# GDN stage: the solve's second product goes out through ScalarE, and the output's low half moves behind the solve's last sums on VectorE

## Chip, core and metric
One Trainium2 chip, one of its NeuronCores. The metric is the time of one execution on the device in microseconds (us), as the median of several runs; lower is better. Engines in the profile: PE is TensorE's matmul and PEld its weight load, DVE is VectorE, ACT is ScalarE, POOL is GpSimd, SP is SyncE, which issues the loads.

## What is computed
Two blocks of a language model run one after the other on a sequence of 512 tokens of width 1024, in float32. The change touches one mixer of the second block, the gated delta rule (GDN), with 8 query and key heads and 16 value heads of width 128 and chunks of 64 tokens:

```python
L = where(strict, einsum(kb, k) * decay, 0)
T = triangular_solve(eye + L, eye)         # a 64 x 64 unit lower triangle for each head and chunk
u, w = T @ vb, T @ (kb * exp(g))
for each chunk:
    v_new = u_n - w_n @ state
    o     = q_n @ state + a_n @ v_new
    state = state * gl_n + k_n^T @ v_new
y = (rmsnorm(o, norm_w) * silu(z)) @ w_out
```

## The kernel before
All float32 products with weights are made from a high and a low half (fp32r): hi x hi, hi x lo, lo x hi. The weights come in blocks of 128 x 1024; SyncE loads a block, ScalarE makes its high half (`split_hi`, L261), VectorE the low one (`split_lo`, L267). The output of the mixer is split in the same way before it is multiplied with `a_w_out`: ScalarE writes `o_hi` (`high`, L2819), VectorE `o_lo` (`low`, L3017 to L3020).

The GDN stage goes through the 8 query/key heads in turns: one "first", six "mid" and one "last" (`gdn_turns`, L2397). Each engine has its own list of instructions for a turn, in an order written out by hand, and the engines meet at semaphores whose values the class `Steps` counts: `Steps.done(name)` raises, `Steps.after(name, turn)` is what another engine waits for. The names in a list must come in the order in which the engine does them.

A turn (j) computes, beside its own head, parts of two others: VectorE and ScalarE prepare the next head's convolution (`conv`, L2966 and L2722), and from the second turn on the head before (p) is normed, gated, split (`normed`, `gated`, `high`, `low`) and multiplied with the output weights (`out_tile` on TensorE, L2515, and on VectorE, L2979). TensorE's large products of the projections (L281) and of the output (L2526 to L2528) are cut into units that a table, `GDN_BESIDE` (L2344), puts behind the small products of the solve, so that TensorE has work while the other engines evict a result. The solve has these steps, `a` being the lower 64 partitions and `b` the upper ones, each product 32 or 48 matmul records of 64 x 64 (`halves`, L2490, all recorded under L2495):
- `f` into the first banks (4 and 7), `g` into the second banks (5 and 6), one after the other; behind them the units of "c" (a quarter of a projection in the middle turns, nothing in the last).
- ScalarE copies `f` out (`fa`, `fb`), VectorE `g` (`ga`, `gb`, L3092), and then adds the identity to the same banks (`ha`, `hb`).
- `f2` needs `fb` and `gb`. ScalarE copies one half of it (`f2a`), VectorE the other (`f2b`, L3096).
- `v` needs `f2a` and `f2b`; VectorE adds it to `ha` and `hb` (`va`, `vb`, L3103). In the last turn output unit O0 follows `v`; in the middle turns two projection units do.
- `y` needs `vb`; behind it come, in the middle turns, a projection unit and O0; then `at` and the four 128-token steps of the recurrence.

O0 is the first output unit, and waits for `lo_1`, the end of `low` (L2519). `low` waits for ScalarE's `high`. On VectorE `low` stands between `f2b` and `va`; ahead of `ga` stand the next head's first convolution and `gated`. Helpers record their callers' instructions under one line: `tt` is L3030 on VectorE, `run` is L2826 on ScalarE.

The lines that order VectorE around the solve:

```python
pe("g")                                                     # L3090
... ga, gb: dve.tensor_copy(G.m[r, :], src[r])              # L3092
... ha, hb: bank + identity
pe("f2"); f2b; splits("vc")
if p is not None: low(p)                                    # L3099
pe("v"); own("hb"); va, vb                                  # L3103
splits("f"); conv(1), conv(2); pe("at")
```

Of the kernel before, what the change touches and what calls it, by code (L numbers as in the profile page):

```python
# [6 lines left out]
ACT = mybir.ActivationFunctionType  # L7
# [5 lines left out]
P = 128  # L13
# [104 lines left out]
def first_and_second_block(nc, a, out):  # L118

    with ExitStack() as ctx:  # L120
        def sem(name):
            return ctx.enter_context(nc.semaphore(name))
# [1246 lines left out]
        class Gla:  # L1369
            b0, t0 = BASE["gla"]  # L1370
            a_lr = tile("gla_a_lr", 8)
            q, k, v, g = ([gla_qkvg[:, n * T:n * T + T] for n in range(n0, n1)] for n0, n1 in ((0, 2), (2, 4), (4, 8), (8, 12)))
            u = [tile(f"gla_u{n}", (21, 30, 31, 32)[n]) for n in range(4)]
            zb, az, cum, rel = ([tile(f"gla_{n}{m}", 33 + 2 * k + m) for m in range(2)]
                                for k, n in enumerate(("zb", "az", "cum", "rel")))
# [10 lines left out]
            pe = Steps(sem("gla_pe"), ["z0", "z1", "vt0", "vt1", "kt0", "kt1", "vt2", "kv00", "kv01", "vt3", "sc0", "sc1", "sc2", "kv10", "kv11", "sc3",  # L1386
                                       "o0", "o1", "sum0", "sum1", "o2", "pw3", "pw2", "o3", "sum2", "sum3", "pw1", "pw0"])
# [443 lines left out]
        class Dsa:  # L1831
# [12 lines left out]
            p, pT = [tile(f"dsa_p{m}", 8 + m) for m in range(4)], [tile("dsa_pT0", 45), sumsq]  # L1844
# [7 lines left out]
            pe = Steps(sem("dsa_pe"), ["sw_kk", "sw_qi0", "sw_qi1", "wt"] + [f"is{t}{h}" for t in range(1, TT) for h in range(IDX_HEADS)]  # L1852
                       + ["vt0", "vt1"])
# [432 lines left out]
        class Gdn:  # L2286
            b0, t0 = BASE["gdn"]
            o_hi, o_lo = ([tile(f"gdn_o_{n}{h}", k + h, dt=F32R) for h in range(2)] for n, k in (("hi", 0), ("lo", 2)))
            gb, dec, eg_row = ([tile(f"gdn_{n}{h}", k + h) for h in range(2)] for n, k in (("gb", 4), ("dec", 6), ("eg_row", 8)))
# [73 lines left out]
        class GdnNext:  # L2363

            pe = Steps(sem("gdn_next_pe"), ["sums"])
# [16 lines left out]
        class GdnTurn:  # L2382
# [4 lines left out]
                       + [n for t in range(TT) for n in (both([f"ks{t}"]) if t else []) + both([f"vn{t}"])  # L2387
                          + [f"{n}{t}_{h}" for h in range(2) for n in (["o", "ds"] if t < TT - 1 else ["o"])]]
                       + ["sums"])
            act = Steps(sem("gdn_act"), ["kc", "vc_0", "vc_1", "fa", "fb", "f2a", "c", "y", "bt", "ct"]  # L2390
                        + [n for t in range(TT) for n in both([f"vn{t}"])] + both(["sq", "oc"]))
            dve = Steps(sem("gdn_dve"), both(["m", "in", "E", "at"]) + [f"{n}{k}" for k in range(GDN_STEPS) for n in ("ta", "tb")]
                        + ["P", "PT", "ga", "gb", "ha", "hb", "f2b", "va", "vb", "at"]
                        + [n for t in range(TT) for n in (both([f"r{t}"]) if t else []) + (both([f"s{t}"]) if t < TT - 1 else [])])
            pool = Steps(sem("gdn_pool"), both(["qd"]) + ["eye"] + both(["kd"]))

# [17 lines left out]
        def first(h):  # L2414
            return bank[(4, 7)[h]]

        def second(h):
            return bank[(5, 6)[h]]
# [60 lines left out]
        def gdn_pe(pe, run):  # L2479
# [81 lines left out]
            def turn(j, p, i, at):  # L2561
# [45 lines left out]
                halves("f", (first(0)[a], half_of(G.X, a), of_E(a, a)), (first(1)[b], half_of(G.X, b), of_E(b, b)))  # L2607
                halves("g", (second(0)[a], of_E(a, a), half_of(G.X, a)), (second(1)[b], of_E(b, b), half_of(G.X, b)))
                beside("c")
                act("fb")  # L2610
                dve("gb")
                halves("f2", (first(0)[a], half_of(G.m, a), half_of(G.F, a)), (first(1)[b], half_of(G.m, b), half_of(G.F, b)),
                       (first(0)[b], half_of(G.X, a), of_E(a, b)))
                beside("f2")
# [88 lines left out]
        def gdn_act(act, after):  # L2703
# [117 lines left out]
            def turn(j, p, i, at):  # L2821
                pe, dve, pool, own = ((lambda n, S=S: act.wait_ge(*S.after(n, j))) for S in (H.pe, H.dve, H.pool, H.act))
                odd, more = 1 - gdn_odd(at), at.kind != "last"

                def run(step, out, src, f, **kw):
                    act.activation(out, src, f, **kw).then_inc(*H.act.done(step))  # L2826

                def splits(point):
                    for n in GDN_SPLITS[at.kind].get(point, "").split():
                        split(at, i, n)  # L2830

                def halves(x):
                    return x.rearrange("p (c x) -> p c x", x=INV_PART)
                if p is not None:
                    inverse_roots(p)
                pe("kt")
                run("kc", G.k_tok[:], second(0)[:], ACT.Copy)
                splits("start")
                for h in range(2):
                    pe(f"vt_{h}")  # L2840
                    run(f"vc_{h}", G.v_tok[h][:], second(1 - h)[:], ACT.Copy)
                splits("vc")
                if p is not None:
                    for h in range(2):
                        gate(h, *gdn_gate(at, i, h)[:3])
                if more:
                    pool("qd_1")
                    conv(0, j + 1, i, at, odd)
                    conv(1, j + 1, i, at, odd)
                a, b = slice(0, P // 2), slice(P // 2, P)  # L2850
                pe("f")
                run("fa", G.F[a, :], first(0)[a], ACT.Copy)
                run("fb", G.F[b, :], first(1)[b], ACT.Copy)
                splits("f")
                pe("f2")
                run("f2a", G.F2[a, :], first(0)[a], ACT.Copy)
                run("c", G.CY[a, :], first(0)[b], ACT.Copy)
                if more:
                    silu(0, i, at, odd)
                    conv(2, j + 1, i, at, odd)  # L2860
                if p is not None:
                    high(p)
                splits("f2")
                pe("y")
                run("y", G.CY[b, :], first(0)[b], ACT.Copy)
                run("bt", G.T[b, :, b], halves(first(1)[b]), ACT.Copy)
                if more:
                    silu(1, i, at, odd)
                    squares(j + 1, odd, p)
                    conv(3, j + 1, i, at, odd)  # L2870
                else:
                    for h in range(2):
                        gate(h, at.through(f"z{h}", i), at.bank(f"z{h}"), (tile_free, BANKS + at.tile[f"z{h}"]))
                pe("at")
                run("ct", G.T[a, :, b], halves(first(1)[a]), ACT.Copy)
                if more:
                    sums(j + 1)
                for t in range(TT):
                    if not more and t == TT - 1:
                        act.preload_act_table_set("natural_log_exp_and_others")  # L2880
                    for h in range(2):
                        pe(f"vn{t}_{h}")
                        if t >= 2:
                            pe(f"o{t - 2}_{h}")
                            pe(f"ds{t - 2}_{h}")
                        run(f"vn{t}_{h}", G.W1[h][:, (1 + t % 2) * P:(2 + t % 2) * P], first(h)[:, (t % 2) * P:(t % 2) * P + P], ACT.Copy,
                            scale=G.beta[:, bass.ds((j * 2 + h) * TT + t, 1)])
                    splits(f"vn{t}")
                    if more and t == 0:
                        for u in (2, 3):  # L2890
                            silu(u, i, at, odd)
                    if more and t == 1:
                        act.preload_act_table_set("natural_log_exp_and_others")
                        roots(j + 1)
                        decays(j + 1)
                    if more and t == 2:
                        gate_rows(j + 1)
                for h in range(2):
                    pe(f"o{TT - 1}_{h}")
                    run(f"sq_{h}", G.W3[h][:], second(h)[:], ACT.Square)  # L2900
                for h in range(2):
                    if more:
                        act.wait_ge(*N.pool.after("n_q", j + 1))
                    run(f"oc_{h}", G.sq[h][:], second(h)[:], ACT.Copy, scale=par[:, R_GDNN:R_GDNN + 1])
                splits("end")
# [18 lines left out]
        def gdn_dve(dve):  # L2924
# [92 lines left out]
            def low(p):  # L3017
                for h in range(2):
                    dve.wait_ge(*GdnOut.act.after(f"hi_{h}", p))
                    dve.tensor_tensor(G.o_lo[h][:], G.sq[h][:], G.o_hi[h][:].bitcast(F32), ALU.subtract).then_inc(*GdnOut.dve.done(f"lo_{h}"))  # L3020

            def turn(j, p, i, at):
# [3 lines left out]
                def done(step):  # L3026
                    return H.dve.done(step)

                def tt(step, out, x, y, op):
                    dve.tensor_tensor(out, x, y, op).then_inc(*done(step))  # L3030

                def splits(point):
                    for n in GDN_LOWS[at.kind].get(point, "").split():
                        split(at, i, n)
# [53 lines left out]
                if p is not None:  # L3088
                    gated(p, [gdn_gate(at, i, h)[3] for h in range(2)])
                pe("g")  # L3090
                for n, r, src in (("ga", a, second(0)), ("gb", b, second(1))):
                    dve.tensor_copy(G.m[r, :], src[r]).then_inc(*done(n))  # L3092
                for n, r, src in (("ha", a, second(0)), ("hb", b, second(1))):
                    tt(n, halves(G.V1[r, :]), halves(src[r]), eye(r), ALU.add)
                pe("f2")
                dve.tensor_copy(G.F2[b, :], first(1)[b]).then_inc(*done("f2b"))  # L3096
                splits("vc")
                if p is not None:
                    low(p)  # L3099
                pe("v")  # L3100
                own("hb")
                for n, r, src in (("va", a, second(0)), ("vb", b, second(1))):
                    tt(n, G.V[r, :], G.V1[r, :], src[r], ALU.add)  # L3103
                splits("f")
                if more:
                    conv(1, j + 1, i, at, odd)
# [870 lines left out]
```

## Time and profile before

| | |
|---|---|
| median of 3 runs | 2735.11 us (2734.95 to 2738.89) |
| the profiled execution's own time | 2736.56 us |
| its span, first to last instruction | 2734.8 us |
| mean granted TensorE clock | 0.998 of full speed |
| busy: TensorE, VectorE, ScalarE, GpSimd | 98%, 65%, 47%, 33% of the span |
| GDN stage's turns | about 1865 to 2389 us of the span |

How to read it: the span is what the profile covers; the device time is 1.8 us longer. "Busy" says how much of the span an engine has an instruction in flight; a matmul counts as busy from its start to its modelled end, so consecutive ones overlap. The chain that ended last is followed back from the last instruction through whatever released each step, and so shows whose time adds up to the span. In a timeline each row has the start, the length and the instruction; "x2" is two merged instructions, and the bracket is the idle time of the engine ahead of it with the releaser that the semaphores suggest. "issue" is idle time for which the profile names no releaser.

### The profile page before, as it was taken

To read this page: it belongs to the slowest core of one execution; us is meant where nothing else is said; L and a number is where in the kernel's file an instruction comes from. 1 tells how busy PE (TensorE), PEld (TensorE's weight loads), DVE (VectorE), ACT (ScalarE), POOL (GpSimd) and SP (SyncE) were. 2 spreads that over 40 slices of the span, in tenths; PEclk is the share of its full clock that TensorE was granted. 3 is DMA by queue.
4 is the path that set the end of the run, shared out by engine and by line. 5 is a ranking of instruction groups with operands and counts; after the bars stand their busy time and mean duration, and the time that the engine had idled before them with its cause. 6 is when DMAs were issued, how large, how long until landed. Compare 5 with 4: busy or idle time off the path is not lost.

```text
span 2734.8 us, 40987 instructions
## 1 busy us (share of the span) xinstructions
PE 2681.2 (98%) x15550; PEld 2223.8 (81%) x15550; DVE 1787.3 (65%) x2641; ACT 1274.7 (47%) x2008; POOL 899.6 (33%) x751
## 2 busy tenths in 40 slices
PE   8999999999999999999999999999999999899998
PEld 6998888789888898887788998877777777777777
DVE  7974336569753687635956887348777777676664
ACT  4542232445323453223554543345555555467775
POOL 5520013136431264403733545104422222122232
PEclk9999999999999999999999999999999999999999
DMA  5343332223553325533213256322222222122222
GB/s 144 87 123 93 96 82 78 82 80 101 170 159 94 96 85 157 175 96 85 78 31 90 83 145 181 106 70 71 78 70 70 70 70 63 44 78 65 66 62 70
DMA packets 484876, 255.94 MB, mean 94 GB/s; under 512 B 17843, under 2 KB 478422, under 8 KB 484710
## 3 DMA queue, kind: packets, MB, share of 16 engines
q1 hardware_dynamic: 484534, 253.40, 32.4%
q8 instruction: 111, 1.82, 0.3%
q14 instruction: 55, 0.45, 0.1%
q10 hardware_dynamic: 176, 0.27, 0.0%
HBM read 251.51 MB, written 2.13 MB: 93 GB/s over the span
## 4 chain that ended last, share of the span: by engine, by line
PE 89%; DVE 6%; ACT 2%; issue 1%; POOL 1%; DMA 0%; SPq 0%; DVEq 0%; ACTq 0%; POOLq 0%
PE bank L281 60%; PE bank L978 12%; PE bank L2495 1%; PE bank L2526 1%; PE bank L2528 1%; DVE w_lo L267 1%; PE bank L2527 1%; DVE dsa_work L2191 1%; PE bank L3435 1%; PE bank L3427 1%; DVE small L2185 1%; PE bank L2640 1%; PE bank L3460 1%; DVE gdn_blocks L3030 1%; PE bank L1569 1%
## 5 line engine op out<-in xcount | busy, mean ns | idle before, releaser
L267 DVE TENSOR_TENSOR w_lo<-w_raw,w_hi 128x1024 fp32r<-128x1024 f32 x365 | 463.1, 1271 | 463.2 <-ACT w_hi L261 443.8
L281 PE MATMUL bank<-x_hi,w_hi 128*128 128x512 f32 x1808 | 737.7, 408 | 6.0 <-DVE w_lo L267 4.2
L281 PE MATMUL bank<-x_lo,w_hi 128*128 128x512 f32 x1808 | 707.8, 391 | 0.6 <-DVE x_lo L623 0.6
L281 PE MATMUL bank<-x_hi,w_lo 128*128 128x512 f32 x1808 | 707.5, 391 | 0.0
L261 ACT ACTIVATE w_hi<-w_raw 128x1024 fp32r<-128x1024 f32 x349 | 366.9, 1056 | 489.7 <-PE bank L281 440.7
L281 PEld LDWEIGHTS bank<-x_hi,w_hi 128*128 128x128 f32 x1808 | 340.4, 188 | 88.1 <-issue 16.5
L281 PEld LDWEIGHTS bank<-x_hi,w_lo 128*128 128x128 f32 x1808 | 340.1, 188 | 74.3
L281 PEld LDWEIGHTS bank<-x_lo,w_hi 128*128 128x128 f32 x1808 | 341.1, 189 | 68.1 <-DVE x_lo L623 3.9
L468 POOL TENSOR_TENSOR sumsq<-sumsq,sq 128x512 f32<-128x512 f32 x56 | 90.3, 1613 | 711.8 <-ACT sq L456 711.2
L281 PE MATMUL bank<-h_hi,w_hi 128*128 128x512 f32 x768 | 300.3, 391 | 0.0
L281 PE MATMUL bank<-h_hi,w_lo 128*128 128x512 f32 x768 | 299.0, 389 | 0.0
L281 PE MATMUL bank<-h_lo,w_hi 128*128 128x512 f32 x768 | 298.8, 389 | 0.0
L281 PEld LDWEIGHTS bank<-h_hi,w_hi 128*128 128x128 f32 x768 | 144.2, 188 | 30.6
L281 PEld LDWEIGHTS bank<-h_hi,w_lo 128*128 128x128 f32 x768 | 144.2, 188 | 30.5
L281 PEld LDWEIGHTS bank<-h_lo,w_hi 128*128 128x128 f32 x768 | 144.2, 188 | 29.4
L978 PE MATMUL bank<-t_hi,w_hi 128*128 128x256 f32 x512 | 146.1, 285 | 0.7 <-DVE w_lo L1192 0.7
L978 PE MATMUL bank<-t_lo,w_hi 128*128 128x256 f32 x512 | 144.8, 283 | 0.0
L978 PE MATMUL bank<-t_hi,w_lo 128*128 128x256 f32 x512 | 144.8, 283 | 0.0
L716 POOL TENSOR_TENSOR sumsq<-sumsq,ada_hi 128x512 f32<-128x512 f32 x48 | 62.1, 1293 | 160.9 <-DVE ada_hi L702 160.9
L978 PE MATMUL bank<-x_hi,w_hi 128*128 128x256 f32 x384 | 109.2, 284 | 0.3
L978 PE MATMUL bank<-x_lo,w_hi 128*128 128x256 f32 x384 | 108.7, 283 | 0.0
L978 PE MATMUL bank<-x_hi,w_lo 128*128 128x256 f32 x384 | 108.6, 283 | 0.0
(542 smaller groups left out, 5070.1 us busy)
## 6 DMA issues: line engine op xcount, KB each, us to landing
w_raw<-in_ffn_wi_dram SPq DMA_DIRECT2D x176, 512.0 KB, 3.8
w_raw<-in_ffn_wo_dram SPq DMA_DIRECT2D x64, 512.0 KB, 3.5
w_raw<-in_ada_w_dram SPq DMA_DIRECT2D x48, 512.0 KB, 4.8
w_raw<-in_a_w_in_dram SPq DMA_DIRECT2D x48, 512.0 KB, 4.0
w_raw<-in_b_w_in_dram SPq DMA_DIRECT2D x32, 512.0 KB, 4.0
w_raw<-in_ffn_wo_dram SPq DMA_DIRECT2D x32, 384.0 KB, 3.1
w_raw<-in_even_w_in_dram SPq DMA_DIRECT2D x16, 512.0 KB, 4.0
w_raw<-in_a_w_out_dram SPq DMA_DIRECT2D x16, 512.0 KB, 3.5
```

The lines of the kernel that those rows point to most:

```text
L261: act.activation(w_hi[b % SPLIT][:], w_raw[raw % RAW][:], ACT.Copy).then_inc(w_hi_done, 1)
L267: dve.tensor_tensor(w_lo[s][:], w_raw[raw_of(b) % RAW][:], w_hi[s][:].bitcast(F32), ALU.subtract).then_inc(w_lo_done, 1)
L281: mm = pe.matmul(out, lhs[:, w], rhs(kt), start=first and kk == 0 and m == 0, stop=last and kk == len(kts) - 1 and m == 2)
L468: pool.tensor_tensor(sumsq[:], sumsq[:], sq[k % 2][:], ALU.add).then_inc(sum_added, 1)
L716: pool.tensor_tensor(dst, x, y, ALU.add).then_inc(ada_added, 1)
L978: mm = pe.matmul(out, lhs[:, w], rhs[:, k, :], start=first and k == 0 and m == 0, stop=k == 3 and m == 2, skip_group_check=True)
L1569: pe.matmul(out[:], w_hi[b % SPLIT][:, w], h_hi[:, x], start=first and kt == kts[0], stop=False)
L2185: dve.max(S.top8, w).then_inc(*s.done(f"top{t}_{k}"))
L2191: dve.match_replace(w, S.top8, w, TAKEN).then_inc(*s.done(f"out{t}_{k}"))
L2495: mm = pe.matmul(out[:, c * INV_PART:(c + 1) * INV_PART], lhs(c), rhs(c), start=True, stop=True)
L2526: pe.matmul(out[:], w_hi[s][:, x], G.o_hi[h][:], start=h == 0, stop=False)
L2527: pe.matmul(out[:], w_hi[s][:, x], G.o_lo[h][:], start=False, stop=False)
```

## The change
ScalarE, not VectorE, copies the product `g` out of its banks: `ga` and `gb` follow `fa` and `fb` on ScalarE. TensorE waits for the one semaphore value `gb` of ScalarE ahead of `f2`. VectorE waits for ScalarE's `gb` ahead of `ha`. On VectorE `low` moves from ahead of `va` to behind `vb`.

```diff
--- before.py
+++ after.py
@@ -2387,10 +2387,10 @@
                        + [n for t in range(TT) for n in (both([f"ks{t}"]) if t else []) + both([f"vn{t}"])
                           + [f"{n}{t}_{h}" for h in range(2) for n in (["o", "ds"] if t < TT - 1 else ["o"])]]
                        + ["sums"])
-            act = Steps(sem("gdn_act"), ["kc", "vc_0", "vc_1", "fa", "fb", "f2a", "c", "y", "bt", "ct"]
+            act = Steps(sem("gdn_act"), ["kc", "vc_0", "vc_1", "fa", "fb", "ga", "gb", "f2a", "c", "y", "bt", "ct"]
                         + [n for t in range(TT) for n in both([f"vn{t}"])] + both(["sq", "oc"]))
             dve = Steps(sem("gdn_dve"), both(["m", "in", "E", "at"]) + [f"{n}{k}" for k in range(GDN_STEPS) for n in ("ta", "tb")]
-                        + ["P", "PT", "ga", "gb", "ha", "hb", "f2b", "va", "vb", "at"]
+                        + ["P", "PT", "ha", "hb", "f2b", "va", "vb", "at"]
                         + [n for t in range(TT) for n in (both([f"r{t}"]) if t else []) + (both([f"s{t}"]) if t < TT - 1 else [])])
             pool = Steps(sem("gdn_pool"), both(["qd"]) + ["eye"] + both(["kd"]))
 
@@ -2607,8 +2607,7 @@
                 halves("f", (first(0)[a], half_of(G.X, a), of_E(a, a)), (first(1)[b], half_of(G.X, b), of_E(b, b)))
                 halves("g", (second(0)[a], of_E(a, a), half_of(G.X, a)), (second(1)[b], of_E(b, b), half_of(G.X, b)))
                 beside("c")
-                act("fb")
-                dve("gb")
+                act("gb")
                 halves("f2", (first(0)[a], half_of(G.m, a), half_of(G.F, a)), (first(1)[b], half_of(G.m, b), half_of(G.F, b)),
                        (first(0)[b], half_of(G.X, a), of_E(a, b)))
                 beside("f2")
@@ -2851,6 +2850,9 @@
                 pe("f")
                 run("fa", G.F[a, :], first(0)[a], ACT.Copy)
                 run("fb", G.F[b, :], first(1)[b], ACT.Copy)
+                pe("g")
+                run("ga", G.m[a, :], second(0)[a], ACT.Copy)
+                run("gb", G.m[b, :], second(1)[b], ACT.Copy)
                 splits("f")
                 pe("f2")
                 run("f2a", G.F2[a, :], first(0)[a], ACT.Copy)
@@ -3088,19 +3090,18 @@
                 if p is not None:
                     gated(p, [gdn_gate(at, i, h)[3] for h in range(2)])
                 pe("g")
-                for n, r, src in (("ga", a, second(0)), ("gb", b, second(1))):
-                    dve.tensor_copy(G.m[r, :], src[r]).then_inc(*done(n))
+                act("gb")
                 for n, r, src in (("ha", a, second(0)), ("hb", b, second(1))):
                     tt(n, halves(G.V1[r, :]), halves(src[r]), eye(r), ALU.add)
                 pe("f2")
                 dve.tensor_copy(G.F2[b, :], first(1)[b]).then_inc(*done("f2b"))
                 splits("vc")
-                if p is not None:
-                    low(p)
                 pe("v")
                 own("hb")
                 for n, r, src in (("va", a, second(0)), ("vb", b, second(1))):
                     tt(n, G.V[r, :], G.V1[r, :], src[r], ALU.add)
+                if p is not None:
+                    low(p)
                 splits("f")
                 if more:
                     conv(1, j + 1, i, at, odd)
```

## Rows read from the trace of the kernel before

**Rows 1.** The page's chain that ended last, share of the span by engine.
```profile
PE 89%; DVE 6%; ACT 2%; issue 1%; POOL 1%; DMA 0%; SPq 0%; DVEq 0%; ACTq 0%; POOLq 0%
```

**Rows 2.** Waits in the GDN stage: engine line, releaser; us in total, times, longest.
```profile
PE bank L2495 <- issue: 7.6, 6, 1.6
...
PE bank L2495 <- DVE gdn_W L3030: 1.8, 6, 0.3
```

**Rows 3.** TensorE's timeline, a middle turn: start us, length us, instruction, idle before.
```profile
2015.34 0.40 PE L281 MATMUL bank<-x_hi,w_lo 128*128 128x512 f32 x1
2016.93 0.27 PE L2495 MATMUL bank<-gdn_W,gdn_W 64*64 64x64 f32 x2 [1.20 <-issue]
...
2019.28 0.40 PE L281 MATMUL bank<-x_hi,w_lo 128*128 128x512 f32 x1
2019.61 1.15 PE L2495 MATMUL bank<-gdn_W,gdn_W 64*64 64x64 f32 x32
...
2023.31 0.39 PE L281 MATMUL bank<-x_hi,w_lo 128*128 128x512 f32 x1
2024.01 0.24 PE L2495 MATMUL bank<-gdn_W,gdn_W 64*64 64x64 f32 x1 [0.31 <-DVE gdn_W L3030]
...
2026.60 0.39 PE L2526 MATMUL bank<-gdn_o_hi,w_hi 128*128 128x512 f32 x1
```

**Rows 4.** VectorE's timeline, the same stretch.
```profile
2015.43 1.40 DVE L3092 COPY gdn_W<-bank 64x512 f32<-64x512 f32 x2
2016.87 1.41 DVE L3030 TENSOR_TENSOR gdn_W<-bank,ident 64x512 f32<-64x512 f32 x2
2018.19 0.69 DVE L3096 COPY gdn_W<-bank 64x512 f32<-64x512 f32 x1
...
2021.13 1.29 DVE L3020 TENSOR_TENSOR gdn_o_lo<-gdn_sq,gdn_o_hi 128x512 fp32r<-128x512 f32 x2 [1.00 <-ACT gdn_o_hi L2819]
2022.46 1.40 DVE L3030 TENSOR_TENSOR gdn_W<-gdn_W,bank 64x512 f32<-64x512 f32 x2
```

**Rows 5.** ScalarE's timeline, the same stretch.
```profile
2013.25 1.21 ACT L2826 ACTIVATE gdn_W<-bank 64x512 f32<-64x512 f32 x2 [4.48 <-PE bank L2495]
2014.49 1.06 ACT L261 ACTIVATE w_hi<-w_raw 128x1024 fp32r<-128x1024 f32 x1
2018.14 1.21 ACT L2826 ACTIVATE gdn_W<-bank 64x512 f32<-64x512 f32 x2 [2.59 <-PE bank L2495]
...
2020.48 1.14 ACT L2819 ACTIVATE gdn_o_hi<-gdn_sq 128x512 fp32r<-128x512 f32 x2
```

**Rows 6.** Pieces of the chain of waits, first turn and a middle one.
```profile
1885.70 3.11 PE bank L2495 x64
1888.81 2.08 PE bank L281 x6
...
2012.13 2.01 PE bank L2495 x64
```

**Rows 7.** Waits in the GDN stage, the two that the first turn has too.
```profile
PE bank L2495 <- DVE gdn_P L3076: 3.0, 2, 2.2
...
PE bank L2495 <- DVE gdn_W L3096: 1.7, 2, 0.9
```

**Rows 8.** Timelines of TensorE, VectorE and ScalarE, last turn.
```profile
2358.22 0.27 PE L2495 MATMUL bank<-gdn_W,gdn_W 64*64 64x64 f32 x2 [1.55 <-DVE gdn_W L3092]
...
2360.27 1.15 PE L2495 MATMUL bank<-gdn_W,gdn_W 64*64 64x64 f32 x32 [0.89 <-DVE gdn_W L3096]
2362.58 0.47 PE L2526 MATMUL bank<-gdn_o_hi,w_hi 128*128 128x512 f32 x1 [1.16 <-issue]
...
2361.19 1.29 DVE L3020 TENSOR_TENSOR gdn_o_lo<-gdn_sq,gdn_o_hi 128x512 fp32r<-128x512 f32 x2 [1.02 <-ACT gdn_o_hi L2819]
...
2355.78 1.21 ACT L2826 ACTIVATE gdn_W<-bank 64x512 f32<-64x512 f32 x2 [11.30 <-PE bank L2495]
```

**Rows 9.** Busy us of each engine and TensorE's granted clock (PEclk), one stretch.
```profile
core 0: us, PE busy (x) PEld busy (x) DVE busy (x) ACT busy (x) POOL busy (x), PEclk, DMA share, GB/s
1887.00:1888.00 1.00, 1.00 (x24) 1.00 (x23) 0.75 (x1) 0.84 (x2) 1.00 (x1) 0.50 0.07 16
```


## The prediction

> **What bounds the kernel now.** I read first the page's chain of waits by engine: TensorE has 89% of the span [rows 1], so a microsecond counts only where TensorE stands idle. Then I read, for the GDN stage, who waited for whom: before the lines of the solve's small products (L2495) TensorE is idle six times for 7.6 us under the name "issue" and six times for 1.8 us behind VectorE's L3030 [rows 2]. Third, the timelines of the three engines through one middle turn. There are eight turns (first, six middle ones, last), and the six middle ones repeat this pattern.
>
> On TensorE the last matmul of the work beside "c" starts at 2015.34, and f2 only at 2016.93, 1.20 us idle; later y starts at 2024.01, 0.31 us idle [rows 3]. In the same stretch VectorE copies ga and gb from 2015.43 to 2016.83, that is, late, because the convolution and the gating stand ahead of them, and f2 starts 0.10 us after gb [rows 3, 4]. So I read "issue" here as the wait for gb. The second idle stretch: va and vb end at 2023.86 and y starts 0.15 us later; they are late because `low` stands ahead of them and itself waits 1.00 us for ScalarE's high half [rows 3, 4]. ScalarE was done with fb at 2014.46 and, but for one weight split, is idle until f2 is through at 2018.1 [rows 5].
>
> **Step 1, ga and gb on ScalarE (middle turns).** Two VectorE copies of 0.70 us go; two ScalarE copies of the same shape come. That form is in the trace: fa and fb take 1.21 us together [rows 5]. f and g together end at 2012.13 + 2.01 = 2014.14, before fb ends [rows 5, 6], so nothing is waited for and gb is done at 2014.46 + 1.21 = 2015.67. With 0.10 to 0.15 us for the wake-up (what rows 3 and 4 show from VectorE; from ScalarE to this product no row shows it, so bounds 0.0 and 0.3) f2 starts at 2015.8. Unhindered it would start 0.33 after the last matmul beside it has started, as v does (2019.61 after 2019.28), at 2015.67 [rows 3]. Gain 16.93 - 15.8 = 1.1 us. In the first middle turn the idle time is 1.6 instead of 1.2 (the longest in [rows 2]) and ScalarE is as early there, so 1.5. Together 5 x 1.1 + 1.5 = 7.0 us.
>
> What is queued behind on ScalarE: the weight split of 1.06 us goes from 2014.49 to 2015.7, ends at 2016.8, and f2a, which needs f2's end at about 2016.95, loses nothing. silu, the copy beside it and `high` follow f2a as before, so the high halves end at 21.62 - 1.1 = 2020.5 [rows 5]. Who waits for gb on VectorE: the two additions ha and hb, now from 2015.75 instead of 2016.87, end 2017.15; f2b until 2017.85 [rows 4]. TensorE reaches v at 19.61 - 1.1 = 2018.5, so v isn't held, with 0.65 us to spare.
>
> The Trainium skill speaks against this move: "ScalarE: Activation LUTs", section Rules for kernel authors, sends simple elementwise operations (maximum, addition, product) to VectorE and budgets about 0.3 us plus 0.83 ns per element for a ScalarE instruction. An estimate from that page is 0.72 us for 512 elements, 1.45 for the two, where this trace has 1.21 for the two.
>
> **Step 2, `low` behind va and vb (middle turns).** v now ends at 2018.5 + 1.15 = 2019.65; VectorE has ended its weight split (2018.88 to 2020.13 before, 1.25 us, now from 2017.85) at 2019.1 and waits for v 0.6 us. va and vb: 2019.7 to 2021.1. TensorE reaches y, without a wait, at 0.33 after the matmul that started 2023.31, less 1.1: 2022.55 [rows 3, 4]. So y's whole delay goes, 24.01 - 23.64 = 0.37 us, six times: 2.2 us. `low` runs from 2021.1, the high halves being there since 2020.5, to 2022.4, where it ended at 2022.42 before. The first output product, which needs it, starts at 26.60 - 1.5 = 2025.1 [rows 3], 2.7 us later. Everything that VectorE has behind (a weight split, two convolutions, the copy of `at`) begins at 2022.4 instead of 2023.86, 1.5 us earlier, as much as TensorE gains, so no later wait opens. GpSimd, which waits for vb, starts the next decays earlier and is off the path. No DMA is added; SyncE's loads wait for the splits that come no later. Middle turns: 7.0 + 2.2 = **9.2 us gained**.
>
> **Step 3, the first turn.** No `low`, no gating, and the work beside "c" hides ga and gb either way. What is idle there is 0.85 us before v, behind f2b, which follows f2 itself [rows 7]. Zero: the cover is the six matmuls, 1.6 us and more; without it the price would be as in the last turn, 0.1 us.
>
> **Step 4, the last turn.** Nothing stands beside "c" there and no convolution ahead of ga, so VectorE copies as soon as g is done, and f2 starts at 2358.22. ScalarE ends fb at 2355.78 + 1.21 = 2356.99, so gb ends at 2358.2 and f2 starts at 2358.3: 0.1 us lost instead of anything gained [rows 8]. And here the first output product follows v directly. Now it waits 1.16 us for `low`, which ends at 2362.48, and starts at 2362.58. In the changed order: v ends at 2360.27 + 0.1 + 1.15 = 2361.5, va and vb take 1.40 as in the middle turns (to 2363.0), `low` 1.29 (to 2364.35), the product starts at 2364.45 [rows 4, 8]. y then follows it directly. **1.9 us lost**, all on the path.
>
> **Step 5, TensorE's clock in the last turn.** The idle time between v and that product grows to 64.45 - 61.5 = 2.9 us. In the first turn TensorE was idle for 2.2 us before f [rows 7], and then the granted clock went to 0.50 of full speed (1.2 instead of 2.4 GHz) [rows 9]. The price is in the chain of waits: f and g took 3.11 instead of 2.01 us and the six matmuls beside them 2.08 instead of 15.74 - 14.14 = 1.60 [rows 3, 6], together 1.6 us. None of the idle times of 1.2 to 1.6 us had this effect. With 2.9 us I take the fall as likely, at 1.5 us, since a part of the slow stretch may lie in the idle time. Bounds: 0 (no fall) and 1.6; a gain is excluded, as a clock can't be granted above full.
>
> **Sum.** 9.2 - 1.9 - 1.5 = 5.8 us gained. The profiled execution (2736.56 us, span 2734.8) becomes 2730.8; the median of the runs, 2735.1, becomes **2729.3 us**, 0.21% less. A measurement of this kernel tells about 0.2% (5.5 us) from no change, so the forecast lies just beyond that bound.
>
> With the Trainium skill's budget ("ScalarE: Activation LUTs", Rules for kernel authors) gb would end at 2015.9 and f2 start at 2016.0: 0.25 us less in each middle turn and the last, 1.7 us in all.
>
> **Rivals.**
> (a) The clock doesn't fall in the last turn: 9.2 - 1.9 = 7.3 gained, 2727.8 us. For it: the last turn of before has three idle stretches of 0.9 to 1.6 us, one after another, which kept f2, v and the product at their usual pace [rows 8]. Against it: 2.9 us is longer than the 2.2 that went before a fall. 22%.
> (b) The change doesn't do what it says in the middle turns: the 1.20 us is TensorE's own issue, as the view names it, or v is held by f2b so that the lead is gone before v. Then only y's 2.2 us are won and 3.4 lost: 2736.3 us. Against it: in the last turn the same idle time is put to VectorE's copy, with the same pattern [rows 2, 8]. 10%.
> (c) ScalarE is no faster at ga and gb than VectorE is: 1.40 us for the two instead of 1.21 [rows 4, 5]. Then gb ends 0.2 us later in the six middle turns and the last one, 1.3 less gained, 2730.6 us. Against it: the same shape from the same kind of bank, fa and fb, takes 1.21. 4%. The Trainium skill's budget, in the section named above, would be a case of this rival, with the 1.7 us given beside the sum.
> (d) Slower: in the middle turns `low` is now behind v, and the first output product waits for `low` as it does in the last turn. From rows, 2.7 us lie between. If VectorE comes to `low` more than 2.7 us later than worked out (because the high halves are late on ScalarE behind ga and gb), TensorE stands in each of six turns. It decides from 2.7 + (9.2 - 3.4) / 6 = 3.7 us on; at 5 us late, 6 x 2.3 - 5.8 = 8 us lost, 2743 us. Against it: `high` ends half a microsecond before VectorE asks. 4%.
> The forecast has 60%.
>
> **The numbers.** Range 2725.8 to 2733.0 us: from (a) less 2 us for the wake-up's lower bound and the scatter of the median (the runs lie between 2734.95 and 2738.89), to 2729.3 with (c), the wake-up at 0.3 (1 us) and the same scatter; (b) and (d) are left out, 14%, and some of the tails. Faster by over 0.2%: all but a little of (a), and somewhat over half of the forecast, which is 0.3 us beyond the bound: 0.54. Within 0.2%: the rest of it, (b) and (c): 0.42. Slower: 0.04.
>
> **What the changed profile would show.** Step 1: no idle time over 0.2 us before f2 in the middle turns, four ScalarE copies in a row, VectorE's L3092 gone. Step 2: none before y, `low` without the 1.00 us of waiting. Each middle turn is 1.5 us shorter. Step 4: 2.9 us idle before L2526 in the last turn, where 1.16 was. Step 5: a granted clock of 0.50 just behind it. Wrong would be: an idle stretch that is new in the middle turns, before v or before L2526, or an "issue" of 1.2 us that stays.

## The result and the profile after

The change made the kernel slower: 2741.43 us median (2740.71 to 2744.14, 16 runs) against 2736.39 us for the kernel before (16 runs); ratio 1.0019 with a 95% interval of 1.0013 to 1.0026. The profiled span grew from 2734.8 to 2739.1 us. The predicted 2729.3 us and the range up to 2733.0 are missed.

Where the 4.3 us of span are, in the profiled executions, by the starts of three matmul groups (the second turn's and the last turn's product kk, L2485, and the sum of squares behind the stage, L503):

| | before | after | predicted change |
|---|---|---|---|
| up to the second turn's kk | 1924.17 | 1923.67 | 0 |
| six middle turns, each | 68.80 | 69.03 | -1.5 |
| last turn, kk to L503 | 66.40 | 69.90 | +3.4 |
| from there to the end | 331.4 | 331.4 | 0 |

The last turn came out as worked out. The middle turns should have given 9.2 us and cost 1.4. The page's chain that ended last, as in [rows 1], shows where to look: VectorE's share grew from 6% to 10% and TensorE's fell.

```profile
PE 87%; DVE 10%; issue 1%; ACT 1%; POOL 1%; DMA 0%; SPq 0%; DVEq 0%; POOLq 0%; ACTq 0%
```

The waits in the GDN stage (as [rows 2]: us in total, times, longest):

```profile
PE bank L2634 <- DVE gdn_W L3142: 5.4, 7, 0.9
...
PE bank L2526 <- issue: 2.9, 1, 2.9
...
PE bank L2526 <- DVE gdn_kT L2975: 1.9, 6, 0.3
...
PE bank L2639 <- ACT gdn_T L2825: 1.2, 6, 0.2
```

The two groups of [rows 2], f2's six stretches of 7.6 us and y's six of 1.8, are gone. In their place TensorE is idle at three points of each middle turn: ahead of output unit O1 (L2526), where it waits for VectorE's convolution of k; ahead of the first tile's product (L2639), where it waits for one of ScalarE's copies into the tile T; and ahead of the second tile's (L2634; the seventh time is in the first turn), where it waits for VectorE's copy of the state. One middle turn on TensorE, as in [rows 3]:

```profile
2027.63 0.50 PE L2526 MATMUL bank<-gdn_o_hi,w_hi 128*128 128x512 f32 x1 [0.31 <-DVE gdn_kT L2975]
...
2030.61 0.68 PE L2639 MATMUL bank<-gdn_v_tok,gdn_T 128*128 128x128 f32 x4 [0.21 <-ACT gdn_T L2825]
...
2035.79 0.71 PE L2634 MATMUL bank<-gdn_W,gdn_kT 128*128 128x128 f32 x4 [0.82 <-DVE gdn_W L3142]
```

0.31 + 0.21 + 0.82 us are idle here, where 1.20 + 0.31 were. That is less, and still the turn is 0.23 us longer: a bracket counts from the modelled end of the last matmul and leaves out that the first ones behind it come slower (the second of O1's matmuls starts 0.33 us after the first, the third 0.24 after the second). By the starts of the matmuls, against the same turn of experiment 3, which has none of these waits, the three points put what follows back by 0.5, 0.4 and 0.8 us, 1.7 in sum; the two of the kernel before by 1.1 and 0.4, 1.5 in sum.

ScalarE did what was expected. As in [rows 5], but with the two new copies behind the two old ones, it does four in 2.45 us from 2012.73 with no wait between them, and the high halves end at 2020.0:

```profile
2012.73 2.45 ACT L2825 ACTIVATE gdn_W<-bank 64x512 f32<-64x512 f32 x4 [4.48 <-PE bank L2495]
...
2018.86 1.14 ACT L2818 ACTIVATE gdn_o_hi<-gdn_sq 128x512 fp32r<-128x512 f32 x2
```

VectorE in the same stretch, to be read against [rows 4]:

```profile
2015.28 1.41 DVE L3032 TENSOR_TENSOR gdn_W<-bank,ident 64x512 f32<-64x512 f32 x2 [0.27 <-ACT gdn_W L2825]
...
2019.18 1.40 DVE L3032 TENSOR_TENSOR gdn_W<-gdn_W,bank 64x512 f32<-64x512 f32 x2 [0.64 <-PE bank L2495]
2020.62 2.38 DVE L3022 TENSOR_TENSOR gdn_o_lo<-gdn_sq,gdn_o_hi 128x512 fp32r<-128x512 f32 x2
2022.92 2.31 DVE L267 TENSOR_TENSOR w_lo<-w_raw,w_hi 128x1024 fp32r<-128x1024 f32 x1
2025.26 2.32 DVE L2975 SCALAR_TENSOR_TENSOR gdn_kT<-bank,par,gdn_kT 128x511 f32<-128x511 f32 x3
```

Up to vb all is on the forecast's schedule: ha and hb wait 0.27 us for gb, v is waited for 0.64 us (0.6 was said), va and vb take 1.40. Then `low` (L3022) takes **2.38 us for its two instructions, not 1.29**, and the weight split behind it **2.31, not 1.23**. That is 2.17 us of VectorE in each middle turn, against a lead of 1.5. What runs beside them is GpSimd, in whose timeline the decays of the next head (`front`, released by vb) begin 0.04 us after `low`:

```profile
2020.66 3.48 POOL L3172 TENSOR_TENSOR gdn_dec<-gdn_gb,not_above 128x512 f32<-128x512 f32 x2 [23.82 <-DVE gdn_W L3032]
2024.10 3.02 POOL L3175 TENSOR_TENSOR gdn_dec<-gdn_dec,gdn_cols 128x512 f32<-128x512 f32 x2
```

In the kernel before the same instructions of GpSimd and VectorE stood like this:

```profile
2023.94 3.58 POOL L3171 TENSOR_TENSOR gdn_dec<-gdn_gb,not_above 128x512 f32<-128x512 f32 x2 [26.57 <-DVE gdn_W L3030]
2027.49 2.03 POOL L3174 TENSOR_TENSOR gdn_dec<-gdn_dec,gdn_cols 128x512 f32<-128x512 f32 x2
...
2023.89 1.23 DVE L267 TENSOR_TENSOR w_lo<-w_raw,w_hi 128x1024 fp32r<-128x1024 f32 x1
2025.15 2.31 DVE L2973 SCALAR_TENSOR_TENSOR gdn_kT<-bank,par,gdn_kT 128x511 f32<-128x511 f32 x3
```

There the split had begun 0.05 us ahead of GpSimd and kept its 1.23 us; it was GpSimd's first instruction that was stretched (2.32 us of the 3.58 for the two; the median of the stage's sixteen is 1.29). And behind the split came the convolutions, which read one operand from a bank and one from SBUF, and ran beside GpSimd at their usual 2.31 us for three. The change put `low`, both of whose inputs are in SBUF, between vb and the split.

The last turn, as in [rows 8] and [rows 9]:

```profile
2361.40 1.15 PE L2495 MATMUL bank<-gdn_W,gdn_W 64*64 64x64 f32 x32 [0.92 <-DVE gdn_W L3097]
2365.41 0.69 PE L2526 MATMUL bank<-gdn_o_hi,w_hi 128*128 128x512 f32 x1 [2.87 <-issue]
...
2366.00:2367.00 1.00, 1.00 (x4) 0.81 (x3) 0.45 (x1) 0.00 (x0) 0.00 (x0) 0.50 0.00 0
```

TensorE was idle 2.87 us between v and O0 (2.9 was forecast), and the granted clock was at 0.50 behind it, from 2365.5 to 2368.9.

### The profile page after: what moved, and what is told of

It is laid out like the page before. It is cut to its first block, busy times and chain, and to the rows that moved or that the text cites. A ratio compares the mean times of both kernels' runs of the same rounds, so it can differ in the third digit from the quotient of the medians.

```text
span 2739.1 us, 40995 instructions
## 1 busy us (share of the span) xinstructions
PE 2684.0 (98%) x15550; PEld 2224.8 (81%) x15550; DVE 1791.6 (65%) x2625; ACT 1284.9 (47%) x2024; POOL 904.5 (33%) x751
## 3 DMA queue, kind: packets, MB, share of 16 engines
HBM read 251.51 MB, written 2.13 MB: 93 GB/s over the span
## 4 chain that ended last, share of the span: by engine, by line
PE 87%; DVE 10%; issue 1%; ACT 1%; POOL 1%; DMA 0%; SPq 0%; DVEq 0%; POOLq 0%; ACTq 0%
PE bank L281 59%; PE bank L978 12%; DVE w_lo L267 2%; DVE gdn_vT L2975 1%; PE bank L2495 1%; DVE dsa_work L2191 1%; PE bank L3436 1%; PE bank L3428 1%; DVE small L2185 1%; PE bank L2526 1%; PE bank L3461 1%; DVE gdn_blocks L3032 1%; PE bank L2528 1%; PE bank L1569 1%; PE bank L2527 1%
## 5 line engine op out<-in xcount | busy, mean ns | idle before, releaser
L267 DVE TENSOR_TENSOR w_lo<-w_raw,w_hi 128x1024 fp32r<-128x1024 f32 x365 | 472.3, 1298 | 461.3 <-ACT w_hi L261 442.1
```

The costliest lines, as they stand in the source:

```text
L267: dve.tensor_tensor(w_lo[s][:], w_raw[raw_of(b) % RAW][:], w_hi[s][:].bitcast(F32), ALU.subtract).then_inc(w_lo_done, 1)
```

## The theories

Theory 1 ("the port" in the expectations): a VectorE instruction with two inputs in SBUF and a GpSimd instruction don't run at the same time; the one that comes second waits until the other has ended. The runs can show this wait, not the circuit behind it. Theory 2: the copies that ScalarE took over stretch what stands beside them, or hold up ScalarE's queue. The experiments take one half of the change at a time, and move only the moment at which GpSimd is released. In the kernel as it stands the first turn releases GpSimd's decays by `PT`, an earlier point, so their data allow any later one.

Turn lengths (us) are read as in the table above, each from the one profiled execution; the median is over all runs, and the ratio is to the runs of the kernel before on the same chip.

| kernel | median us | ratio, 95% interval | middle turn | last turn |
|---|---|---|---|---|
| before | 2736.39 | | 68.80 | 66.40 |
| the change | 2741.43 | 1.0019 (1.0013 to 1.0026) | 69.03 | 69.90 |
| e1 copies only | 2729.68 | 0.9972 (0.9962 to 0.9983) | 67.64 | 66.67 |
| e2 low only | 2747.78 | 1.0038 (1.0025 to 1.0052) | 70.16 | 70.37 |
| e3 GpSimd behind low | 2732.24 | 0.9981 (0.9972 to 0.9990) | 67.23 | 71.33 |
| e4 last turn as before | 2739.35 | 1.0006 (0.9997 to 1.0015) | 68.99 | 66.64 |
| e5 both repairs | 2728.92 | 0.9972 (0.9962 to 0.9982) | 67.23 | 68.52 |
| e6 before, GpSimd early | 2743.17 | 1.0024 (1.0014 to 1.0034) | 69.87 | 66.38 |
| e7 split ahead of low | 2743.19 | 1.0020 (1.0011 to 1.0029) | 69.01 | 71.40 |
| e8 GpSimd behind at | 2735.05 | 0.9992 (0.9983 to 1.0001) | 67.98 | 69.88 |
| e9 = e5 again | 2728.42 | 0.9966 (0.9954 to 0.9978) | 67.22 | 68.45 |
| e10 = e1 again | 2730.40 | 0.9975 (0.9966 to 0.9985) | 67.59 | 68.83 |

## Experiment 1: only the copies move

The edit, against the changed kernel:

```diff
                 splits("vc")
+                if p is not None:
+                    low(p)
                 pe("v")
...
                     tt(n, G.V[r, :], G.V1[r, :], src[r], ALU.add)
-                if p is not None:
-                    low(p)
```

> Only the first half of the change: ga and gb on ScalarE, low stays ahead of va. Theory 1 (the port): in the middle turns the moved low lets GpSimd's decays, released by vb, start together with low, and VectorE's instructions with two inputs in SBUF and GpSimd's wait for each other, 2.2 us in each middle turn. Here vb is followed by the weight split as before, so no instruction of VectorE is stretched: low 1.29 us, the split 1.23; the middle turn is 1.1 to 1.2 us shorter than 68.7, f2's idle time is gone, y's 0.3 stays; the last turn is as before within 0.1 us. In all 7 to 7.5 us less than before, 2729 us. Theory 2 (the copies on ScalarE stretch what stands beside them, or hold its queue so that the high halves and the squares come late): low and the split are stretched here too, and the time is that of before or above, 2736 us or more.

Measured: 2729.68 us, middle turn 67.64, as theory 1 had it. VectorE, GpSimd and TensorE in a middle turn:

```profile
2018.62 1.29 DVE L3022 TENSOR_TENSOR gdn_o_lo<-gdn_sq,gdn_o_hi 128x512 fp32r<-128x512 f32 x2 [0.97 <-ACT gdn_o_hi L2818]
...
2021.38 1.23 DVE L267 TENSOR_TENSOR w_lo<-w_raw,w_hi 128x1024 fp32r<-128x1024 f32 x1
...
2021.43 3.57 POOL L3172 TENSOR_TENSOR gdn_dec<-gdn_gb,not_above 128x512 f32<-128x512 f32 x2 [25.48 <-DVE gdn_W L3032]
...
2021.50 0.24 PE L2495 MATMUL bank<-gdn_W,gdn_W 64*64 64x64 f32 x1 [0.31 <-DVE gdn_W L3032]
```

`low` takes 1.29 us and the split 1.23, with ScalarE's copies in place: the copies stretch neither. The split has begun when GpSimd is released, and y keeps its 0.31 us. ScalarE's half of the change is worth 68.80 - 67.64 = 1.16 us in each middle turn.

## Experiment 2: only low moves

The edit, against the kernel before:

```diff
                 splits("vc")
-                if p is not None:
-                    low(p)
                 pe("v")
...
                     tt(n, G.V[r, :], G.V1[r, :], src[r], ALU.add)
+                if p is not None:
+                    low(p)
```

> Only the second half of the change: low behind vb, ga and gb stay on VectorE. Theory 1 (the port): low takes 2.4 instead of 1.3 us and the split behind it 2.3 instead of 1.2, and without the lead that ScalarE's copies gave, the convolution of k starts 1.8 us later than before against TensorE; the middle turns are 1.5 us or so longer than 68.7, and the last turn loses its 3.4 us: 2736.4 + 9 + 3.4 = 2749 us. Theory 2 (ScalarE's copies are at fault): low and the split keep 1.3 and 1.2 us, the middle turns gain y's 0.37 us, the last loses 3.4: 2737.6 us.

Measured: 2747.78 us, the middle turn 1.36 us longer than before. VectorE's `low` and split:

```profile
2023.63 2.38 DVE L3020 TENSOR_TENSOR gdn_o_lo<-gdn_sq,gdn_o_hi 128x512 fp32r<-128x512 f32 x2
2025.94 2.30 DVE L267 TENSOR_TENSOR w_lo<-w_raw,w_hi 128x1024 fp32r<-128x1024 f32 x1
```

These are the same 2.4 and 2.3 us as with the full change. So it is `low`'s new place that stretches both, and theory 2 falls: ScalarE's queue is that of the kernel before here.

## Experiment 3: the full change, GpSimd released behind low

```diff
-                    dve("PT" if p is None else "vb")
+                    pool.wait_ge(*(H.dve.after("PT", j) if p is None else GdnOut.dve.after("lo_1", p)))
```

> The full change, and GpSimd's decays of the next head wait for the end of low instead of vb in the middle turns, nothing else. Theory 1 (the port): VectorE is in the weight split when GpSimd begins, as before; low 1.29 us, split 1.23, the middle turn 1.5 us shorter than 68.7; with the last turn's 3.4 us the time is 5.8 us below that of before, 2730.6 us. Theory 2: GpSimd's start doesn't matter, 2741 us as with the full change.

Measured: 2732.24 us; the middle turn is 67.23 us, 1.57 less than before, where the forecast's steps 1 and 2 gave 1.53. VectorE and GpSimd:

```profile
2018.44 1.29 DVE L3022 TENSOR_TENSOR gdn_o_lo<-gdn_sq,gdn_o_hi 128x512 fp32r<-128x512 f32 x2
2019.65 1.22 DVE L267 TENSOR_TENSOR w_lo<-w_raw,w_hi 128x1024 fp32r<-128x1024 f32 x1
...
2019.81 3.47 POOL L3172 TENSOR_TENSOR gdn_dec<-gdn_gb,not_above 128x512 f32<-128x512 f32 x2 [25.15 <-DVE gdn_o_lo L3022]
```

One release of GpSimd, 1.3 us later behind vb, gives back 1.80 us in each middle turn. The median is 1.6 us above the expected one, and the last turn shows why: it was 71.33 us, 1.4 more than with the full change, with the granted clock lowered from 2349.6 to 2359.8, about 10 us, instead of 3.4 us with the full change. It fell before TensorE's 2.87 us of idle time there (2352.2 to 2355.0), behind the 1.69 us ahead of f2.

## Experiments 4 and 5: the last turn

```diff
                 splits("vc")
+                if not more:
+                    low(p)
                 pe("v")
...
-                if p is not None:
+                if p is not None and more:
                     low(p)
```

This is e4; e5 adds the line of e3.

> The full change, but in the last turn low keeps its place ahead of va. Both theories: the last turn's idle time of 2.87 us before the first output product goes back to 1.2, and with it the fall of TensorE's clock; 3.4 us less than the full change, 2738.0 us, and the middle turns stay at 69.0 us. If the clock falls in any case, only 1.9 us are won, 2739.5 us.

> The full change with both repairs: GpSimd's decays wait for the end of low in the middle turns, and in the last turn low keeps its place. Theory 1 (the port): the middle turns at 67.2 us, the last as before within 0.2 us; 9 us less than before, 2727.3 us. Theory 2 (ScalarE's copies): 2738 us, as with the last turn repaired alone.

e4: 2739.35 us; the last turn 66.64 us, 3.26 less than with the full change, the middle turns 68.99. But its profiled execution (2736.82 us) is the fastest of 11, 2.5 us below their median, and by the median e4 has only 2.9 of the 3.4 us back that were expected (2.1 us above the kernel before on its chip, where the full change was 5.0 above it on its own). The granted clock of the slower runs, 0.997 to 0.998, is no lower than the profiled one's 0.997, so what makes them slower isn't shown.

e5: 2728.92 us, the middle turns 67.23, but a last turn of 68.52. Its rows:

```profile
2349.02 0.27 PE L2495 MATMUL bank<-gdn_W,gdn_W 64*64 64x64 f32 x2 [1.69 <-ACT gdn_W L2825]
...
2351.09 1.97 PE L2495 MATMUL bank<-gdn_W,gdn_W 64*64 64x64 f32 x32 [0.92 <-DVE gdn_W L3097]
2353.38 0.76 PE L2526 MATMUL bank<-gdn_o_hi,w_hi 128*128 128x512 f32 x1 [0.31 <-issue]
...
2351.00:2352.00 1.00, 0.91 (x17) 0.94 (x19) 0.02 (x1) 1.00 (x3) 0.00 (x0) 0.50 0.00 0
```

TensorE was idle for 1.69, 0.92 and 0.31 us in that stretch, none of it as long as the 2.15 us of the first turn, and the granted clock fell all the same: v took 1.97 instead of 1.15 us. So 2727.3 was 1.6 too low.

## Experiment 6: the kernel before, GpSimd released early

```diff
-                    dve("PT" if p is None else "vb")
+                    dve("PT" if p is None else "f2b")
```

> The kernel before, with one edit: in the middle turns GpSimd's decays wait for f2b instead of vb and so run beside the weight split, low and the sums. Theory 1 (the port): at least one of the two instructions of low waits for an instruction of GpSimd of 1.0 to 1.3 us; low takes 1.6 to 2.4 us, va and vb and with them y are late by as much: 0.3 to 1.3 us in each middle turn, 2738 to 2744 us. If GpSimd is only slowed itself, as its first instruction was in the kernel before, low keeps 1.29 us and the time is that of before, 2736.4 us.

Measured: 2743.17 us. Nothing of the change is in this kernel, and its `low` is stretched in the same way:

```profile
2022.41 2.39 DVE L3020 TENSOR_TENSOR gdn_o_lo<-gdn_sq,gdn_o_hi 128x512 fp32r<-128x512 f32 x2 [1.00 <-ACT gdn_o_hi L2819]
2024.84 1.40 DVE L3030 TENSOR_TENSOR gdn_W<-gdn_W,bank 64x512 f32<-64x512 f32 x2
2026.27 1.51 DVE L267 TENSOR_TENSOR w_lo<-w_raw,w_hi 128x1024 fp32r<-128x1024 f32 x1
...
2020.24 4.02 POOL L3171 TENSOR_TENSOR gdn_dec<-gdn_gb,not_above 128x512 f32<-128x512 f32 x2 [21.59 <-DVE gdn_W L3096]
...
2026.39 0.24 PE L2495 MATMUL bank<-gdn_W,gdn_W 64*64 64x64 f32 x1 [1.41 <-DVE gdn_W L3030]
```

GpSimd's first instruction waits for the split that was under way (2.31 us of the 4.02 for the two), the first of `low` runs in 0.69 us, the second waits for GpSimd's second and takes 1.78 (2.39 for the two, overlapping), and TensorE's idle time ahead of y, 0.31 us before, is 1.41: 1.10 more, and the turn is 1.07 us longer, 69.87 us. va and vb, with one input from a bank, keep 1.40 us though GpSimd is at work beside them. This shows the price of the wait with no part of the change in the kernel.

## Experiment 7: the split ahead of low

```diff
-                if p is not None:
-                    low(p)
                 splits("f")
+                if p is not None:
+                    low(p)
```

> The full change with the weight split ahead of low, so that VectorE goes into a split when GpSimd is released, as in the kernel before, but low comes right behind. Theory 1, read closely (VectorE and GpSimd take turns instruction by instruction: the two-input instruction that has begun isn't stretched, each of the two behind it waits for one instruction of GpSimd): the split keeps 1.23 us, low takes 3.5 to 3.8 us instead of 2.4, the sum of the three instructions stays at 4.6 to 5.1 us, the convolution begins no earlier than with the full change, and low now ends 2 us later than there, 0.5 to 1 us too late for the first output product. Middle turns 69.0 to 69.6 us, 2741 to 2745 us. Rival: what counts is only who comes first after vb; then low keeps 1.3 us and the middle turn is 67.2 us, 2731 us.

```profile
2021.85 1.23 DVE L267 TENSOR_TENSOR w_lo<-w_raw,w_hi 128x1024 fp32r<-128x1024 f32 x1
2022.99 3.47 DVE L3022 TENSOR_TENSOR gdn_o_lo<-gdn_sq,gdn_o_hi 128x512 fp32r<-128x512 f32 x2
...
2021.90 4.02 POOL L3172 TENSOR_TENSOR gdn_dec<-gdn_gb,not_above 128x512 f32<-128x512 f32 x2 [23.82 <-DVE gdn_W L3032]
```

Measured: 2743.19 us, middle turn 69.01. The split, which had begun, keeps 1.23 us; `low` takes 3.47 instead of 1.29, 1.76 and 1.79 for its two instructions where one takes 0.69. From the start of the first of the three instructions to the first convolution it is 4.65 us here and 4.64 with the full change. (The last turn, 71.40 us, is longer because `low` is behind the split there too: TensorE is idle for 4.0 us ahead of O0.) So it isn't who comes first that counts, but how many two-input instructions stand behind the first one while GpSimd has work: two here, two with the full change, none before.

## Experiment 8: GpSimd released by at

```diff
-                    dve("PT" if p is None else "vb")
+                    dve("PT" if p is None else "at")
```

> The full change, with GpSimd's decays released by the copy of at instead of vb. Theory 1: low and the split behind vb keep 1.3 and 1.2 us as with the release behind low, but GpSimd's four instructions now meet the two weight splits ahead of the recurrence, which take about 1.3 us more in sum; with little slack ahead of the second tile's product the middle turn is 67.2 + 1 = 68.2 us, 2737 us with the last turn's loss. Rival (only low and the split behind vb have no slack): 67.2 us, 2731 us.

```profile
2019.78 1.29 DVE L3022 TENSOR_TENSOR gdn_o_lo<-gdn_sq,gdn_o_hi 128x512 fp32r<-128x512 f32 x2
...
2029.51 3.52 DVE L267 TENSOR_TENSOR w_lo<-w_raw,w_hi 128x1024 fp32r<-128x1024 f32 x2
...
2029.92 4.01 POOL L3175 TENSOR_TENSOR gdn_dec<-gdn_dec,gdn_cols 128x512 f32<-128x512 f32 x2
```

Measured: 2735.05 us, middle turn 67.98. `low` and its split are unhindered, the two splits ahead of the recurrence take 3.52 us instead of 2.35, and the second tile's product waits 0.68 us for VectorE. The turn is 0.2 us and the median 2 us below what was expected, but far from the rival's 67.2 and 2731: the price moved to where the overlap went, and it ate about half of what e3 gave.

## Experiments 9 and 10: which version is the best

The kernels of e5 and e1 again, beside each other on one chip.

> The same kernel as e5_both, beside e10 on one chip, to tell which version is the best. The middle turns say 67.2 against 67.65 us, so 2.6 us between them if the last turn is the same; in the profile of e5 TensorE's clock fell in the last turn behind idle times of 1.7 and 0.9 us, which would cost this version up to 1.5 us of it. 2727 to 2729 us.

> The same kernel as e1_copies_only, beside e9. 2729 to 2730 us, 1 to 3 us above e9.

They took 2728.42 and 2730.40 us; the ratios are 0.9966 and 0.9975, with intervals that overlap. The middle turns, 67.22 and 67.59, differ by 2.2 us in six. Both beat the kernel before and the change. The full change with both repairs is lower by 2.0 us here and by 0.8 in e5 and e1, which ran on different chips and have the same ratio, 0.9972. So it is the better of the two by its middle turns; by the whole time that isn't clear of the noise.

## Why the prediction was wrong, step by step

**What bounds the kernel:** right. Both idle stretches were what they were taken for, and "issue" was the wait for gb (rival (b) falls): with ScalarE's copies it is gone, in e1 and e3 alike.

**Step 1** (ScalarE's copies, 7.0 us in six turns): right. e1 has 6 x 1.16 = 7.0 us. Rival (c) falls too: four copies took 2.45 us, 0.61 each. The Trainium skill's budget ("ScalarE: Activation LUTs", section Rules for kernel authors), from which the prediction estimated 0.72 us, is stated there for a bias passed as a pointer operand. The call of these copies passes no bias, so that budget wasn't one for them.

**Step 2** (`low` behind vb) failed, in one sentence: "GpSimd, which waits for vb, starts the next decays earlier and is off the path." GpSimd's own work is off the path, but the moment at which it starts isn't without effect on it. The step moved `low` past the instruction that releases GpSimd, and costed it with a duration, 1.29 us, measured where GpSimd was waiting. The missing term is 2.17 us of VectorE in each middle turn; with it the lead of 1.5 us turns into 0.7 us of delay, of which 0.2 us arrive in the turn. With the term taken away (e3) the step's 9.2 us are there: 6 x 1.57 = 9.4.

The sign was in the trace of before: GpSimd's two instructions beside the split took 3.58 us against 1.29 for one of them as the median. The prediction rested on no GpSimd row. VectorE's side of it was there too, in the first turn, beside the second of these two instructions of GpSimd:

```profile
1875.99 0.28 DVE L3030 TENSOR_TENSOR gdn_blocks<-bank,gdn_blocks 128x112 f32<-128x112 f32 x1
1876.30 0.69 DVE L3030 TENSOR_TENSOR gdn_blocks<-gdn_blocks 128x112 f32<-128x112 f32 x1
...
1874.77 2.08 POOL L3193 TENSOR_TENSOR gdn_kdec<-gdn_k_tok,gdn_cols 128x512 f32<-128x512 f32 x2
```

The instruction with one input from a bank keeps 0.28 us; the one with both in SBUF takes 0.69, where the same shape takes 0.27 in the other seven turns. It writes plain float32, so it isn't the fp32r output of `low` and of the split that makes them wait.

The Trainium skill has the rule: "SBUF — State Buffer", section Who interferes with whom, says that a VectorE instruction with two SBUF inputs contends with a GpSimd instruction that reads SBUF, that whoever issues first keeps the shared pair for the whole instruction, and that the other blocks fully. The trace agrees: the first keeps its time, the second takes up to 1.1 us longer, and instructions with one operand from a bank keep theirs.

**Step 3** (first turn, zero): right in its sum; the second turn's kk starts 0.5 us earlier than before, and in the other kernels it starts between 1923.1 and 1924.9. The idle time before v is 0.92 us against 0.85. Two things cancel in this zero: the first kk starts 2.0 us later (1866.0), and in this one profile the granted clock didn't fall behind f's wait, which was 1.68 us long instead of 2.15.

**Steps 4 and 5** (last turn, 1.9 and 1.5 us): right, 3.5 us measured against 3.4, and e4's profile has 3.3 of it back. The bound of 1.6 us for the clock was too low: in e3 the last turn is 71.33 - 66.40 = 4.9 us longer, 3.0 more than the 1.9 of step 4, and the lowered clock lasted three times as long. Rival (a) did not happen in the profiled execution.

**Rival (d)** had the sign and `low` as the place, but not the cause: the high halves weren't late, O0 wasn't what waited with the full change, and GpSimd wasn't in it.

**The forecast's size:** 9.2 - 1.9 - 1.5 = 5.8 us less, against 4.3 more in the profiled span, 10.1 us apart. The missing term makes 6 x (1.53 + 0.23) = 10.6 of it, the last turn 0.1, and the first turn takes 0.5 off. The median is 12.1 us above the forecast: 10.8 for the change, and 1.3 because the forecast started from 2735.1 us, the median of three runs, where sixteen gave 2736.4.

## What to carry to other kernels

When an instruction moves past a semaphore step, list every engine that this step releases, and look at what the released engine runs beside the moved instruction's new place. A duration read in one place holds in another only if the same neighbours run there: for a VectorE instruction with two SBUF inputs, look first at GpSimd's timeline, where a stretched instruction is the trace of a collision that so far costs nothing. A cheap repair is to move the release, not the work. In e3 GpSimd is let go as VectorE enters a split with no other two-input instruction close behind, and each middle turn is 1.80 us shorter than with the change; in e8 it is let go still later, and meets two other splits, which takes 0.75 us of that away.

## What was not expected of the hardware

VectorE and GpSimd take turns: with several instructions queued on both, each two-input instruction of VectorE that found GpSimd at work waited for the rest of one of its instructions, and in none of these rows for two in a row. The wait was 1.1 us in e7 (twice) and with the full change (0.69 and then 1.77 us for the two of `low`, and 2.31 for the split), and 0.3 to 0.7 us where less was left of GpSimd's instruction (e6's split, 1.51 us; e8's two splits, 1.54 and 1.93). Between the full change and e7 the order differs and the total doesn't.

TensorE's granted clock fell to 0.50 (1.2 of 2.4 GHz) in the last turn of e5, e9 and e10, behind idle stretches of 1.7 and 0.9 us, and stayed at full speed in e1 and e4 with the same order of work there; each is one profile, so how often it falls isn't known. In the first turn it fell in eleven of the twelve profiles, behind idle stretches of 2.13 to 2.21 us, and not in that of the full change, behind 1.68. A fall makes a last turn of 66.7 us into 68.5 to 68.8, and together with the 2.87 us of idle time the last turn takes 69.9 to 71.3. It is a part of the scatter left in these kernels' times; a way to keep TensorE busy in the last turn wasn't tried.
